# Loads, stores and one 4 MB row copy put in another order around the gated-linear-attention stage

## The reference

```python
mod = silu(c) @ w_ada + b_ada                  # 9 rows of 6 x 1024: shift, scale, gate, twice
h = rmsnorm(x, g_mix) * (1 + scale) + shift
gq, gk, gv, gr, ga, nq, nkc, nks, nkw, ngate = split(h @ w_in)     # 2856 columns
o = gated_linear_attention(gq, gk, gv, gr, ga, state_gla)          # 4 heads
# native sparse attention: a compressed, a selected and a window branch
rows = concat(cache_cmp[page_table[b]], nkc)   # 1024 past rows of 256 words per sequence
cmp  = blocks_of_32_rows(rows + phi_pe) @ phi_w
y = concat(o, nsa) @ w_out                     # then a top-4-of-32 mixture of experts
new_cmp, new_sel, new_win = nkc, nks, nkw      # returned: the new key and value rows
new_win_sample = concat(state_win, nkw)[:, -512:]   # 504 old rows of each sequence, then 8 new
```

## Time and profile before

| | us |
|---|---|
| median of 3 runs | 1828.37 |
| lowest and highest | 1827.34, 1829.06 |
| time of the profiled execution | 1829.17 |
| span of its profile | 1827.3 |

### The profile page before, as it was taken

The page is one execution under the profiler, slowest core; times in us unless marked ns, Lnnn a source line. Parts: engine busy times, 40 slices in busy tenths (PEclk is TensorE's granted clock), DMA queues, the critical chain, the costliest instruction groups (busy, mean ns, idle before and its releaser), DMA issues.

```text
span 1827.3 us, 27018 instructions
## 1 busy us (share of the span) xinstructions
PE 1684.2 (92%) x9012; PEld 1313.4 (72%) x9012; DVE 1432.6 (78%) x1363; ACT 1106.3 (61%) x1060; POOL 328.7 (18%) x310
## 2 busy tenths in 40 slices
PE   3999967889798779999999999999999999999994
PEld 2776756656554468888888888888888888888873
DVE  4422545477434879999999999999999999999996
ACT  4222324355333356777777777777777777777772
POOL 0000012200011011222312312222231231232110
PEclk9999979799899779999999999999999999999997
DMA  9454384420136378999999999999999999999973
GB/s 348 166 188 166 66 224 148 143 66 2 47 118 185 144 289 313 373 377 375 370 378 380 370 377 377 378 369 377 379 373 380 379 369 383 380 372 371 387 286 123
DMA packets 114598, 516.08 MB, mean 282 GB/s; under 512 B 25870, under 2 KB 47710, under 8 KB 62058
## 3 DMA queue, kind: packets, MB, share of 16 engines
q1 hardware_dynamic: 101082, 483.48, 70.3%
q0 software_dynamic: 12800, 29.45, 5.8%
q10 hardware_dynamic: 656, 2.36, 0.3%
HBM read 502.75 MB, written 31.09 MB: 292 GB/s over the span
## 4 chain that ended last, share of the span: by engine, by line
PE 61%; DVE 2%; ACT 1%; DMA 1%; issue 0%; DVEq 0%; POOL 0%; ACTq 0%; POOLq 0%
PE banks L2934 57%; PE banks L2942 3%; PE banks L2920 1%; DMA ffn_rows<-weighed,block_rows 0%; DVE arena L3205 0%; PE banks L2985 0%; DVE arena L3204 0%; ACT sigmoids L3106 0%; DVE split L3127 0%; ACT split L3038 0%; DMA arena<-ffn_rows 0%; DVE arena L3223 0%; DVEq L2801 0%; ACT final_stat L3107 0%; ACT L3112 0%
## 5 line engine op out<-in xcount | busy, mean ns | idle before, releaser
L2934 PE MATMUL banks<-split 128*128 128x512 f32 x4608 | 1079.1, 393 | 6.9 <-DVE split L3131 5.8
L2934 PEld LDWEIGHTS banks<-split 128*128 128x128 f32 x4608 | 862.8, 189 | 192.6 <-issue 13.7
L3127 DVE TENSOR_TENSOR split<-expert_buffers,split 128x2048 fp32r<-128x2048 f32 x384 | 864.7, 2284 | 44.3 <-ACT split L3038 42.6
L3038 ACT ACTIVATE split<-expert_buffers 128x2048 fp32r<-128x2048 f32 x384 | 733.0, 1918 | 220.8 <-PE banks L2934 216.9
L2873 POOL TENSOR_TENSOR wait_taken<-routing 128x1 f32<-128x1 f32 x62 | 76.1, 1227 | 812.8 <-PE banks L2942 464.3
L2896 POOL DMA_INDIRECT ffn_rows<-weighed,block_rows x31 | 107.7, 3476 | 4.8 <-issue 4.6
L644 PE MATMUL banks<-w_in_high,hT_high 128*128 128x476 f32 x192 | 75.8, 395 | 4.2 <-DVE hT_low L477 4.2
L3131 DVE TENSOR_TENSOR split<-banks,split 128x1024 fp32r<-128x1024 f32 x64 | 77.7, 1214 | 0.7 <-ACT split L3041 0.7
L644 PE MATMUL banks<-w_in_high,hT_low 128*128 128x476 f32 x192 | 73.3, 382 | 0.0
L3041 ACT ACTIVATE split<-banks 128x1024 fp32r<-128x1024 f32 x64 | 64.4, 1007 | 4.2 <-PE banks L2942 4.2
L3063 ACT ACTIVATE weighed<-banks,block_weights 128x1024 f32<-128x1024 f32 x32 | 35.7, 1117 | 45.5 <-PE banks L2934 45.5
(11 more groups left out here) (398 smaller groups left out, 1726.1 us busy)
## 6 DMA issues: line engine op xcount, KB each, us to landing
expert_buffers<-in_w_gate SPq DMA_DIRECT2D x128, 1024.0 KB, 8.3
expert_buffers<-in_w_up SPq DMA_DIRECT2D x128, 1024.0 KB, 6.2
expert_buffers<-in_w_down SPq DMA_DIRECT2D x128, 1024.0 KB, 8.9
arena<-in_w_ada SPq DMA_DIRECT2D x16, 1024.0 KB, 4.8
w_in_landing<-in_w_in SPq DMA_DIRECT2D x5, 1904.0 KB, 16.8
arena<-in_w_ada SPq DMA_DIRECT2D x4, 2048.0 KB, 19.6
arena<-in_x_prompt SPq DMA_DIRECT2D x8, 512.0 KB, 7.2
arena<-in_cache_cmp POOLq DMA_DIRECT2D x32, 128.0 KB, 3.4
```

The costliest lines, as they stand in the source:

```text
L2934: last = pe.matmul(ps[:, bank + c, :], x[:, kt * P:(kt + 1) * P].bitcast(F32R), wt.bitcast(F32R), start=(m == 2 and kt == 0 and x is xs[0] ...
L3038: act.activation(high[:, j % RING_Q].bitcast(F32R), v, ACT.Copy).then_inc(s_high, 1)
L3127: dve.tensor_tensor(rest[:, j % RING_Q].bitcast(F32R), v, high[:, j % RING_Q], ALU.subtract).then_inc(s_rest, 1)
```

## The change

The new version does five things.

1. The loads of `phi_w` move from `gla` to the end of `project`, behind a wait for the last modulation product (they overwrite the two buffers of the modulation weights). `phi_pe` stays in `gla`.
2. In `gla` SP reads the page numbers and loads its first four pages ahead of the stores.
3. The row copy moves from `gla` to the end of SP's list in `prompt_attention`, with a wait for it behind.
4. The modulation's biases are added in two operations on 128 rows instead of eight on 9 rows, and at step 22 instead of 23. For that POOL clears three banks' width of the target instead of one at the start, and the DVE three banks instead of one.
5. In `gla` PE turns `features(0)` first, and `features(1)` ahead of the last part of `queries_and_keys`.

```diff
+def load_phi(core, sp):
+    for h in range(KVH):
+        rows = slice(64 * h, 64 * h + 64)
+        for c in range(2):
+            for u in range(2):
+                sp.dma_start(core.phi[rows, c, :, 64 * u:64 * u + 64],
+                             core.io["phi_w"][0, c, u * GAPS * HD:(u + 1) * GAPS * HD].rearrange("(l d) n -> d l n", d=HD)
+                             ).then_inc(core.s_phi, 16)
...
+            sp.wait_ge(s_mod, 2)
+            load_phi(core, sp)
             sp.wait_ge(s_rest, 16)
-            sp.wait_ge(s_modcp, 9)
+            sp.wait_ge(s_modcp, 3)
...
-            pool.memset(mod[:, 0, :], 0.0).then_inc(s_blank, 1)
+            pool.memset(mod, 0.0).then_inc(s_blank, 1)
...
-            dve.memset(ps[:, ADA, :], 0.0).then_inc(s_blankps, 1)
+            dve.memset(ps[:, ADA:ADA + 3, :], 0.0).then_inc(s_blankps, 1)
...
                 if i == GATE + 6:
+                    dve.wait_ge(s_mod, 2)
+                    for b in (1, 2):
+                        dve.tensor_tensor(mod[:, b, :], mod[:, b, :], ps[:, ADA + b, :], ALU.add).then_inc(s_modcp, 1)
                     for q in range(2, NT):
                         gate_values(q)
-                if i == STEPS - 1:
-                    dve.wait_ge(s_mod, 2)
-                    for b in (1, 2):
-                        for j in range(4):
-                            rows = slice(32 * j, 32 * j + 9)
-                            dve.tensor_tensor(mod[rows, b, :], mod[rows, b, :], ps[rows, ADA + b, :], ALU.add).then_inc(s_modcp, 1)
...
-                        sp.dma_start(core.phi[rows, c, :, 64 * u:64 * u + 64],
-                                     io["phi_w"][0, c, u * GAPS * HD:(u + 1) * GAPS * HD].rearrange("(l d) n -> d l n", d=HD)
-                                     ).then_inc(core.s_phi, 16)
...
+            sp.wait_ge(core.s_pageno, 16)
+            for i, page in page_numbers(core, sp, 0, range(SLOTS // 2)):
+                load_page(core, sp, 0, i, page)
             for o, c in ((2, C_KC), (3, C_KS), (4, C_KW)):
...
-            sp.dma_start(io["out_8"][0, :, 0:SEQ - TS].rearrange("b t c h d -> b (t c h d)"),
-                         io["state_win"][0, :, TS:SEQ].rearrange("b t c h d -> b (t c h d)")).then_inc(core.s_kvout, 16)
-            core.n_kvout = 16 * (6 + NSEQ)
-            sp.wait_ge(core.s_pageno, 16)
-            for i, page in page_numbers(core, sp, 0, range(SLOTS // 2)):
-                load_page(core, sp, 0, i, page)
+            core.n_kvout = 16 * (5 + NSEQ)
...
+            features(0)
             queries_and_keys(2)
-            features(0)
-            for p in range(2):
-                queries_and_keys(p)
-            for t in range(1, NT):
+            queries_and_keys(0)
+            features(1)
+            queries_and_keys(1)
+            for t in range(2, NT):
                 features(t)
...
              for b in range(0, HELD, 2):
                 load_past(core, sp, b, past_numbers(core, sp, b))
+            sp.dma_start(core.io["out_8"][0, :, 0:SEQ - TS].rearrange("b t c h d -> b (t c h d)"),
+                         core.io["state_win"][0, :, TS:SEQ].rearrange("b t c h d -> b (t c h d)")).then_inc(s_old, 16)
+            sp.wait_ge(s_old, 16)
```

More of the change, by code:

```diff
@@ L116, in sem, with keep @@
         return s
+    def keep(self, s):
+        self.sems.remove(s)
+        self.carried.append(s)
     def stage_done(self):
```

13 lines of the change are left out of this document (7 added, 6 removed).

## The result

The changed kernel took 1816.26 us (median of 4 executions, 1811.85 to 1817.36), the kernel before beside it 1828.71 us (4 executions): a ratio of 0.9925, 95% interval 0.9912 to 0.9937 (the quotient of the two medians alone is 0.9932, 12.4 us). Against the 1828.37 us ahead of the prediction the ratio gives 1814.7 us, 13.7 us less, with an interval of 1812.3 to 1816.9, where 1817.5 and a range from 1815.0 to 1822.5 were predicted. The profiled execution took 1816.97 us with a span of 1815.2, which is 12.1 us less than before. Measured once more later, the same kernel gave 0.994 (0.9916 to 0.9964), that is 1817.4 us against the same 1828.37. So the direction is sure, and the size lies between some 11 and 14 us.

What follows compares the result with a forecast made beforehand. The prediction took cache pages late behind the row copy on SP's queue as the bound where the change acts; 9.6 + 0.8 + 0.5 = 10.9 us off 1828.37 gave 1817.5 us, range 1815.0 to 1822.5.

Steps and rivals of the forecast that it cites:

- Pages and copy, 9.6 us: In `compress`, the hole at the first cache tile closes fully: 9.6 us gained, ends 8.5 and 9.9.
- The rival of POOL's late pages: In `compress`, POOL's pages still take 7.1 us to land: gain 6.6 instead of 9.6, total 1820.5 us; chance 0.14.
- within `gla` they saved nothing: Compression weights: nobody waited for them in `gla`, and their loads fit beside the projection, so moving them was costed at nothing.
- set by the order of SP's list: End of the stage with the 9.9 us hole: bound by SP issuing pages behind the row copy, not by a computing engine.
- The border, 0.8: Projection to `gla`: fewer bias operations let SP store the modulation earlier, gaining 0.8 us, between 0 and 0.9.
- The head, 0.5: Start of `gla` to line 884: the new order of transposes gains 0.5 us, ends -0.3 and 0.8.
- Full clock in the first product: Rival: without the hole PE enters `compress`'s first product warm, 17.61 becomes 15.96 us, total 1815.8 us; chance 0.12.
- the same, only earlier: From prompt attention on, everything was to stay the same and only start earlier.
- A later stage that begins with a smaller shift: Sign of being wrong: a stage after the first product starts with a smaller shift than that product has.
- the slower rival: Prompt attention: half clock lasts longer, three more units eat the gain, four end at 1835 us; chance 0.04.
- The other length: Sign of being wrong: the stretch of half clock in prompt attention has another length.
- both small terms: Border and head, 0.8 and 0.5 us; the range's low end put 0.7 on top for their upper ends.

Runs made afterwards that it cites:

- the repeat: The changed kernel measured once more, nothing edited: 0.994 (0.9916 to 0.9964) of the kernel before, that is 1817.4 us.
- identity products: The changed kernel with 38 unread products of the identity with itself on PE, filling idle time ahead of prompt attention: 0.9938 (0.9916 to 0.996).
- no copy: The changed kernel with the row copy left out altogether: 0.9924 (0.991 to 0.9939).

## Why the prediction was right or wrong, point by point

- **Pages and copy, 9.6 us: right in size.** Measured 9.4 in the profile (20.42 for 29.82), 10.3 in the repeat. DVE's first copy came 10.2 us sooner after the stage's start (9.85 predicted), and its chain to the product took 0.75 us longer (0.25 were allowed); that the short waits for pages made it longer is argued. The rival of POOL's late pages fell: they took 3.0 us.
- **The weights, "within `gla` they saved nothing": wrong.** Moved alone they give as much as the whole change, within the noise (0.9937). The sentence asked who waits for the weights, and nobody does. It did not ask what stands behind their eight issues in SP's list: the copy and the pages. Their issues took 5.3 and 6.2 us of SP's time. The sum came out all the same, because the early weights and the moved copy close the same hole and it can be closed only once. Had the change been the weights alone, this step would have predicted nothing and missed 11 us.
- **The hole's cause: the copy ahead of the pages, right; "set by the order of SP's list", half right.** Leaving the copy out closes the hole with everything else in its old place; putting the pages ahead of it, with the copy still in `gla`, only moves the hole to the fifth tile. What counts is the time at which the copy ends against the time at which the pages behind it are wanted.
- **The border, 0.8: right, 0.9.** In every kernel without added products there 1.2 us with early stores and 2.1 with late ones.
- **The head, 0.5: this is the term that was mis-sized, and the step that failed.** The head gained 3.7 us. The order itself gives 0.7 to 0.9. The other 2.8 to 3.0 go with the clock: in the kernel before PE ran at 0.50 from its first transpose on for 6.4 us, in the changed one not at all. The prediction used the half clock only for its low end, -0.3 "if the transposes run at the half clock throughout", and so took for an exception what the kernel before already did (0.50 from 218.5 to 225.0 in the view above); it priced no gain from it. It did weigh the clock for the first product, but not for this stretch. What in the change spared the head the dip stays open: parts 4 and 5 undone singly bring one dip back, but so do the old places of pages and copy, which leave PE's list at the head as it is.
- **Full clock in the first product: the rival came in part.** Its price was right, 15.96 us for the 15.93 that such a product takes. Measured were 17.85 in the first profile, 15.93 in the repeat, 15.93 and 17.61 in the two variants of the changed kernel that leave this place alone (identity products, no copy). The second product, priced at no change, took 15.77 in the first profile and 14.09 in the repeat. So the two together differ by up to 3.6 us between executions of one kernel.
- **From the product on, "the same, only earlier": nearly.** 15.1 us at the product, 12.7 at prompt attention, 12.1 at the end. A later stage that begins with a smaller shift was one of the prediction's own signs of being wrong, and it came.
- **Prompt attention's clock, the slower rival: did not come.** The half clock lasted for 27 us of the stage as before in the first profile and for 35 in the repeat, where the stage took 1.4 to 1.9 us more, not the 17.6 that the rival had. The other length is a sign of being wrong too, by the prediction's list, and it came in the repeat. The copy there costs nothing that shows, as predicted.
- **The range.** The sum of 10.9 stood for a product 10.9 us sooner; with 3.2 more at the head and 1.1 of a projection that ended sooner in this execution it was about 15.1, and 12.1 to 13.7 at the end. The low end allowed 13.4, and 13.7 misses it by 0.3 us. In the trace the head is the one term of the sum that is far off: its upper bound, 0.8, had no clock in it. But the miss itself is smaller than the noise. The first interval, 1812.3 to 1816.9, reaches into the range, the second measurement, 1817.4 us within 1813.0 to 1821.8, falls on the forecast, and the kernels without a hole that had a head of 10.4 to 11.2 us measured 0.9928 to 0.9942, where the changed one had 0.9925 and 0.994. Two slips of the working changed little: the 0.7 added for "both small terms" at the low end holds only 0.4 of theirs and 0.3 of the pages' term, and the experts take 1177 us of the span, not 1190.

## What to carry to other kernels

Of an issue that is moved away, ask not only who waits for its data but what stands behind it on its queue: eight loads that nobody waited for held up the loads that somebody did. Two parts of a change that shorten the same wait are worth the wait once, so try each alone before crediting either; and moving one load ahead of a large transfer can leave the next one behind it. Where a change touches a border, look up the granted clock of the stretch behind it, and price that stretch at both levels.

## What the runs showed of the hardware

- A 4 MB copy within the chip's memory, issued from SP, holds up the later transfers of that queue: pages of 128 KB issued 3.9 to 4.7 us behind it took 20.0 us to land, 19.9 and 20.5 in two other kernels, and 2 to 4 us with no copy ahead. POOL's pages, on another queue, took 7.1 and 10.3 us beside it instead of 3.2.
- PE's clock fell to 1.2 GHz at borders with idle times as short as 1.85 us, and the length of the stretch behind repeated in each of three kernels measured twice (10.45 and 10.46 us; 11.21 and 11.15; 8.85 twice, without a fall), while it differed between kernels with the same idle time. Two kernels with some 1.1 us of extra work in the gap showed no fall; that the shorter idle time is the cause is not shown.
- In the kernel before PE stayed at 1.2 GHz for some 27 us of prompt attention though it was busy for over 90 of 100 (22.67 of 24 us); with 38 products put into the idle time before the stretch it lasted as long (24.18 of 25 us busy).
- Prompt attention takes one of two lengths, 123.4 to 124.0 or 125.2 to 125.5 us, in kernels that are the same there. That, the clock in each product of `compress` and a projection whose last copy ended at 215.65 and 218.32 us in two executions of one kernel make executions differ by several us; a term of 1 us, and even the 3 us of the head, can be read from the trace but not from the time of the whole.
